# Long convolution by tables: input turned in quarters of its times, half of the forward products replaced by sums, inverses moved by a slot

## The chip, the cores and the metric

One core of a Trainium2 chip runs the program. The metric is the device time of one execution in microseconds (us), the median over several runs. The engines are TensorE (PE; its weight loads are shown apart as PEld), VectorE (DVE), ScalarE (ACT), GpSimd (POOL), and SyncE (SP), which here only issues DMA. Each engine works through its own list of instructions in order and waits on semaphores for the others.

## What is computed

One layer of a model with three parallel groups of heads over 512 latent tokens and 256 context tokens, all in float32. The group that the change touches is a gated long convolution of order two over 512 channels:

```python
def fft_long_conv(z, k_f, bias):
    L = z.shape[1]
    zf = z.astype(jnp.float32)
    y = jnp.fft.irfft(jnp.fft.rfft(zf, n=2 * L, axis=1) * k_f, n=2 * L, axis=1)[:, :L]
    return (y + zf * bias.astype(jnp.float32)).astype(z.dtype)
...
    v, x1, x2 = jnp.split(u, 3, axis=-1)
    z = x1 * fft_long_conv(v, k_f[:, 0], lp["hy_bias"][0])
    return x2 * fft_long_conv(z, k_f[:, 1], lp["hy_bias"][1])
```

The other two groups are attention with compressed keys and a pooling over windows. All three read one projection `h @ w_in` (2048 to 4928 columns) and feed one output projection (2048 by 2048).

## The kernel before

**Precision.** Every large product is done in three passes, with each operand cut into a high part (rounded to the type fp32r by ACT) and a low part (the rest, by a subtraction on DVE): high by high, low by high, high by low. `passes` (L1758 to L1761) issues the three matmuls.

**Slots.** The projection runs as 68 chunks of weights of 128 by 1024. The loop variable `n` of every engine counts these chunks, and this document calls the work written down for one `n` a slot. In a slot ACT makes the high part of chunk n + 1 (`chunk_high`, L630), DVE its low part (`chunk_low`, L1151), and PE multiplies chunk n (`half_chunk`, 24 matmuls of 512 columns at L1730): 12, then the slot's extra work, then 12. PE's chunk n waits for the low part of chunk n; ACT's high part of chunk n + 1 waits until PE has finished chunk n - 1. Everything else is put into slots by hand: each engine has its own list of "if n is this, do that", in the order in which it is done.

**The convolution.** For order o (0, 1) and half of the channels (256 of 512 each), m = 2 o + half. With c = n - TC[o] for the first half and n - TC[o] - 4 for the second (TC = 9, 25), the slots are:

- `transposes` (PE, L1834; c = 0, or -2 for the second half): times come onto the partitions. Even and odd times lie in two banks; a source is read with a step of two floats.
- `turned` (ACT and DVE): high and low part of the transposed input.
- `forward` (PE; c = 1, or 0 for the second half): cosine and sine products (x) of the even and the odd times (pr), for 256 frequencies (two blocks ft) from 256 times (two blocks jt): 16 products of three passes, 48 matmuls of 256 columns.
- `odd_parts` (ACT, L737) copies the odd times' products out of PSUM, `butterflies` (DVE, c = 1, L1246 and L1247) adds and subtracts them, which gives the 256 frequencies and the 256 mirrored ones.
- `filtered` (DVE, c = 2) and `mirrored`, `folded` (DVE, c = 3) multiply by the filter's spectrum and fold; `product_high` (ACT, L752) and `product_low` (DVE, L1287), both c = 4, cut the result in two.
- `inverse` (PE; c = 5 and 6) makes the output of 128 channels each, 24 matmuls of 256 columns, and `outputs` (DVE, same slot, L1297 and L1298) adds and multiplies.

So order 0 has transposes in slots 9 and 11, forward in 10 and 13, inverses in 14, 15, 18, 19; order 1 the same 16 slots later. `neighbour_taps` (DVE, L1176 and L1178) is a short convolution that is put into the slots of `NEIGHBOURS`. `link` lets an engine wait for its own last instruction. SP loads the cosine and sine tables (`fwd_raw`, L377) before the chunks from 3 on; ACT and DVE cut them into parts in slots 3 and 4. In slots 4 to 8 and 20 to 24 the filter's taps and spectrum are made.

Of the kernel before, what the change touches and what calls it, by code (L numbers as in the profile page):

```python
# [61 lines left out]
def backbone(nc, mem, t, out):  # L62
# [6 lines left out]
    with ExitStack() as ctx:  # L69
# [6 lines left out]
        cond, silu_c, spread = alloc("cond", 2 * KT), alloc("silu_c", 2 * KT), alloc("silu_spread", 32 * KT)  # L76
# [18 lines left out]

        shift_x, shift_c = at("shift_x", TMP + 0.5, AW), at("shift_c", TMP + 1.75, 3 * P)
# [6 lines left out]
        inv_hi, inv_raw, inv_lo = at("inv_hi", TAB + 8, 1024, F32R), at("inv_raw", TAB + 10, 1024), at("inv_lo", TAB + 10, 1024, F32R)  # L103
        T = at("temps", TMP, 5 * L)
# [214 lines left out]
        def _(eng):  # L319
# [57 lines left out]
            eng.dma_start(fwd_raw[:], t["tables"][:, 0:2048]).then_inc(tab_in, 16)  # L377
            for n in range(KW, 4 * B_GROUPS):
# [15 lines left out]
                if slot == TC[0] + 9:  # L394
                    eng.wait_ge(mirror_done, 2)
                    load_decay(5)
                    load_decay(6)
# [129 lines left out]
        def _(eng):  # L527
# [204 lines left out]
            def odd_parts(n):  # L732
                for x in range(2):
                    eng.wait_ge(f_mm, 2 * n + x + 1)
                    if n and x == 0:
                        eng.wait_ge(g_lo_done, 4 * n)
                    eng.activation(tmp_of(0) if x else tmp_of(2), ps[2 + 2 * x + 1][:], ACT.Copy).then_inc(f_odd, 1)  # L737
# [8 lines left out]
            def product_high(n):  # L746
                for g in range(4):
                    eng.wait_ge(g_sum, 4 * n + g + 1)
                    if n and g == 0:
                        eng.wait_ge(i_mm, 2 * n)  # L750
                    src = (tmp_of(0), Z[:, 2 * L:3 * L], tmp_of(1), Z[:, 3 * L:4 * L])[g]
                    eng.activation(g_hi[:, g * L:(g + 1) * L], src, ACT.Copy).then_inc(g_hi_done, 1)  # L752
# [134 lines left out]
            for n in range(4 * B_GROUPS):  # L887
# [19 lines left out]
                if n == 12:  # L907
                    eng.wait_ge(tab_in, 32)
                    eng.activation(inv_hi[:], inv_raw[:], ACT.Copy).then_inc(fixed_hi, 1)
                if n == 3:  # L910
                    eng.wait_ge(tab_in, 16)
                    eng.activation(fwd_hi[:], fwd_raw[:], ACT.Copy).then_inc(fixed_hi, 1)
                    sine(1)
# [125 lines left out]
        def _(eng):  # L1039
# [141 lines left out]
            def fixed_low(i):  # L1181

                lo, x, hi = ((w3_lo, w3_raw, w3_hi), (fwd_lo, fwd_raw, fwd_hi), (inv_lo, inv_raw, inv_hi), (w3_lo, w3_raw, w3_hi))[i]
                eng.wait_ge(fixed_hi, i + 1)
                eng.tensor_tensor(lo[:], x[:], hi[:], ALU.subtract).then_inc(fixed_lo, 1)
# [54 lines left out]
            def butterflies(n):  # L1240
                for x in range(2):
                    eng.wait_ge(f_odd, 2 * n + x + 1)
                    if n and x == 0:
                        eng.wait_ge(g_hi_done, 4 * n)
                    odd = tmp_of(0) if x else tmp_of(2)
                    eng.tensor_tensor(Z[:, x * L:(x + 1) * L], ps[2 + 2 * x][:], odd, ALU.add)  # L1246
                    eng.tensor_tensor(Z[:, (2 + x) * L:(3 + x) * L], ps[2 + 2 * x][:], odd, ALU.subtract).then_inc(f_done, 1)  # L1247

            def filtered(n):
                half = n % 2  # L1250
                eng.wait_ge(f_done, 2 * n + 2)
                eng.wait_ge(k_done, 4 * (n // 2) + 4)
                c, s = as2(Z[:, 0:L]), as2(Z[:, L:2 * L])
                kc, ks = halves(K, 0, half), halves(K, 2, half)
                ta, tb = as2(tmp_of(0)), as2(tmp_of(1))
# [4 lines left out]
                eng.tensor_tensor(c, c, tb, ALU.subtract)  # L1260
                link(eng.tensor_tensor(s, s, ta, ALU.add))

            def mirrored(n):
                half = n % 2
                c, s = as2(Z[:, 2 * L:3 * L]), as2(Z[:, 3 * L:4 * L])
                kc, ks = halves(K, 4, half), halves(K, 6, half)
                ta, tb = as2(tmp_of(3)), as2(tmp_of(4))
# [7 lines left out]
            def folded(n):  # L1275
                eng.wait_ge(mirror_done, n + 1)
                for x in range(2):
                    low_, mirror = Z[:, x * L:(x + 1) * L], Z[:, (2 + x) * L:(3 + x) * L]
                    eng.tensor_tensor(tmp_of(x), low_, mirror, ALU.add).then_inc(g_sum, 1)
                    eng.tensor_tensor(mirror, low_, mirror, ALU.subtract).then_inc(g_sum, 1)  # L1280

            def product_low(n):
                for g in range(4):
                    eng.wait_ge(g_sum, 4 * n + g + 1)
                    eng.wait_ge(g_hi_done, 4 * n + g + 1)
                    src = (tmp_of(0), Z[:, 2 * L:3 * L], tmp_of(1), Z[:, 3 * L:4 * L])[g]
                    eng.tensor_tensor(g_lo[:, g * L:(g + 1) * L], src, g_hi[:, g * L:(g + 1) * L], ALU.subtract).then_inc(g_lo_done, 1)  # L1287

            def outputs(o, c):
# [5 lines left out]
                y = ps[6 + c % 2][:].rearrange("p (r t) -> p t r", r=2)  # L1295
                z = u(c).rearrange("p (t r) -> p t r", r=2)
                link(eng.scalar_tensor_tensor(out=z, in0=y, scalar=nrm[:, n:n + 1], in1=z, op0=ALU.mult, op1=ALU.add))  # L1297
# [166 lines left out]
            for n in range(4 * B_GROUPS):  # L1464
# [28 lines left out]
                for o in range(2):  # L1493
# [8 lines left out]
                    for half, c in ((0, n - TC[o]), (1, n - TC[o] - 4)):  # L1502
# [3 lines left out]
                        if c == 1:  # L1506
                            butterflies(m)
                        if c == 2:
                            filtered(m)
                        if c == 3:  # L1510
                            mirrored(m)
                            folded(m)
                        if c == 4:
                            product_low(m)
                        if c in (5, 6):
                            outputs(o, 2 * half + c - 5)
# [130 lines left out]
        def _(eng):  # L1647
# [172 lines left out]
            def transposes(n):  # L1820
# [9 lines left out]
                for b in range(2):  # L1830
                    for jt in range(2):
                        for cc in range(2):
                            src = u(2 * half + cc)[:, b + 256 * jt:256 * (jt + 1):2]
# [3 lines left out]
            def forward(n):  # L1837
# [4 lines left out]
                else:  # L1842
                    eng.wait_ge(k_done, 4 * o + 4)
                for x in range(2):
                    for pr in range(2):
                        for ft in range(2):
                            for jt in range(2):
                                a = (2 * (2 * x + pr) + jt) * 256 + ft * P
                                b = (2 * pr + jt) * 256
                                mm = passes(ps[2 + 2 * x + pr][:, ft * 256:(ft + 1) * 256],  # L1850
                                            (fwd_hi[:, a:a + P], fwd_lo[:, a:a + P]),
                                            (zt_hi[:, b:b + 256], zt_lo[:, b:b + 256]), jt == 0, jt == 1)
                    mm.then_inc(f_mm, 1)
# [23 lines left out]
            for n in range(4 * B_GROUPS):  # L1877
# [3 lines left out]
                for o in range(2):  # L1881
# [7 lines left out]
                    for half, c in ((0, n - TC[o]), (1, n - TC[o] - 4)):  # L1889
# [5 lines left out]
                        if c in (5, 6):  # L1895
                            inverse(o, 2 * half + c - 5)
# [243 lines left out]
def layout(inputs):  # L2140
# [13 lines left out]
    def tile(o):  # L2154
# [12 lines left out]

    w = np.pi * (2 * np.arange(HF) + 1) / (2.0 * L)
    waves = [fn(np.outer(2 * np.arange(HF) + odd, w)) for fn in (np.cos, np.sin) for odd in (0, 1)]
    tables = np.concatenate([m[i * P:(i + 1) * P] for m in waves for i in range(2)]  # L2170
                            + [m.T[i * P:(i + 1) * P] for m in waves[::2] for i in range(2)], axis=1)

    f32 = np.float32
    order = np.concatenate([np.arange(0, L, 2), np.arange(1, L, 2)])
# [69 lines left out]
```

## Time and profile before

| | |
|---|---|
| median of 3 runs | 973.11 us (972.97 to 973.54) |
| the profiled execution | 973.39 us |
| its span | 971.6 us |
| granted clock of PE over the span | 0.997 |
| busy: PE, PEld, DVE, ACT, POOL | 944.4, 780.7, 615.5, 397.7, 97.3 us |

A row of the timeline is: start in us, duration in us, engine, line, operation, output and inputs, shapes, count; in brackets the idle time before it and what ended that. Durations of matmuls overlap their successors, so the distance between starts tells what one costs. DVE's rows overlap a little in the same way. In the waits a row reads: who waits, for what, total us, times, longest. In groups: count, busy us, mean ns of one, idle before.

### The profile page before, as it was taken

Reading aid. Unit: us, or ns where it says so; the run is one execution under the profiler, and the core shown is the slowest. Engines: PE = TensorE matmul, PEld = TensorE weight load, DVE = VectorE, ACT = ScalarE, POOL = GpSimd, SP = SyncE. Lnnn points to the kernel's source line nnn. Section 1 sums busy time; section 2 is a strip of 40 time slices with the busy share of each in tenths; the row PEclk is TensorE's granted clock in tenths of the full one; section 3 lists DMA queues with packets and bytes.
Section 4 is the critical chain, followed back from the end, with each engine's and each line's share of the span. In section 5 each row is a group of like instructions: output and inputs, shape, how many; then the busy total and the mean of one; then the engine's idle time right before and its main releaser. Section 6 shows DMA issues by size and latency. Waiting matters only on the chain.

```text
span 971.6 us, 12485 instructions
## 1 busy us (share of the span) xinstructions
PE 944.4 (97%) x5018; PEld 780.7 (80%) x5018; DVE 615.5 (63%) x805; ACT 397.7 (41%) x625; POOL 97.3 (10%) x78
## 2 busy tenths in 40 slices
PE   5999999999999999999999999999999999999996
PEld 3667777888888889888887788889888888888885
DVE  2766889788756676736785563777777754414254
ACT  3555656354234433323323323645455542212224
POOL 1122200210002200000002360000000000202020
PEclk9999999999999999999999999999999999999998
DMA  9999833222232221258775233101001127222314
GB/s 368 420 422 375 333 128 98 68 84 68 85 96 84 73 78 52 87 167 297 264 283 172 87 129 131 38 18 44 12 1 44 44 88 295 94 87 87 107 67 173
DMA packets 28982, 137.21 MB, mean 141 GB/s; under 512 B 3739, under 2 KB 4059, under 8 KB 21756
## 3 DMA queue, kind: packets, MB, share of 16 engines
q1 hardware_dynamic: 28204, 135.76, 38.9%
q8 instruction: 40, 0.66, 0.3%
q10 hardware_dynamic: 720, 0.65, 0.2%
q14 instruction: 18, 0.15, 0.0%
HBM read 132.20 MB, written 4.19 MB: 140 GB/s over the span
## 4 chain that ended last, share of the span: by engine, by line
PE 81%; DVE 9%; DMA 4%; ACT 4%; issue 2%; POOLq 0%; SPq 0%; ACTq 0%; DVEq 0%
PE pp L1730 32%; PE pp L1760 18%; PE pp L2038 18%; DMA wa_raw<-in_wa_dram 3%; PE pp L1677 3%; PE pp L2001 2%; PE pp L1654 2%; DVE w_lo L1151 1%; PE pp L1681 1%; DMA ada_raw<-in_w_ada_dram 1%; PE pp L1993 1%; PE pp L1992 1%; DVE softmax_stats L1411 1%; DVE pt_lo L1426 1%; ACT U L837 1%
## 5 line engine op out<-in xcount | busy, mean ns | idle before, releaser
L1730 PE MATMUL pp<-h_hi,w_hi 128*128 128x512 f32 x544 | 214.2, 394 | 1.9 <-DVE w_lo L1151 1.2
L1730 PE MATMUL pp<-h_hi,w_lo 128*128 128x512 f32 x544 | 211.9, 390 | 0.0
L1730 PE MATMUL pp<-h_lo,w_hi 128*128 128x512 f32 x544 | 211.9, 389 | 0.0
L1151 DVE TENSOR_TENSOR w_lo<-w_raw,w_hi 128x1024 fp32r<-128x1024 f32 x68 | 87.3, 1284 | 98.4 <-ACT w_hi L630 98.2
L630 ACT ACTIVATE w_hi<-w_raw 128x1024 fp32r<-128x1024 f32 x68 | 71.9, 1058 | 168.2 <-PE pp L1730 120.7
L1730 PEld LDWEIGHTS pp<-h_hi,w_hi 128*128 128x128 f32 x544 | 102.2, 188 | 26.3 <-DVE w_lo L1151 3.6
L1730 PEld LDWEIGHTS pp<-h_hi,w_lo 128*128 128x128 f32 x544 | 102.1, 188 | 21.6
L1730 PEld LDWEIGHTS pp<-h_lo,w_hi 128*128 128x128 f32 x544 | 102.2, 188 | 20.8 <-issue 0.5
L2038 PE MATMUL pp<-wo_hi,m_hi 128*128 128x512 f32 x256 | 100.5, 393 | 0.0
L2038 PE MATMUL pp<-wo_hi,m_lo 128*128 128x512 f32 x256 | 99.6, 389 | 0.0
L2038 PE MATMUL pp<-wo_lo,m_hi 128*128 128x512 f32 x256 | 99.6, 389 | 0.0
L1446 DVE TENSOR_TENSOR wo_lo<-wo_raw,wo_hi 128x2048 fp32r<-128x2048 f32 x16 | 36.7, 2291 | 92.7 <-ACT wo_hi L868 92.7
L868 ACT ACTIVATE wo_hi<-wo_raw 128x2048 fp32r<-128x2048 f32 x16 | 30.6, 1914 | 89.4 <-PE pp L2038 89.4
L2038 PEld LDWEIGHTS pp<-wo_lo,m_hi 128*128 128x128 f32 x256 | 48.1, 188 | 10.4 <-issue 0.5
L2038 PEld LDWEIGHTS pp<-wo_hi,m_hi 128*128 128x128 f32 x256 | 48.1, 188 | 10.3 <-issue 0.5
L2038 PEld LDWEIGHTS pp<-wo_hi,m_lo 128*128 128x128 f32 x256 | 48.0, 188 | 10.1
L519 POOL TENSOR_TENSOR y<-y,gain 128x512 f32<-128x512 f32 x12 | 15.5, 1297 | 339.8 <-ACT out_tmp L875 339.5
L1426 DVE TENSOR_TENSOR pt_lo<-pp,pt_hi 128x768 fp32r<-128x768 f32 x32 | 30.5, 953 | 26.1 <-ACT pt_hi L845 26.0
L845 ACT ACTIVATE pt_hi<-pp 128x768 fp32r<-128x768 f32 x32 | 26.0, 812 | 50.9 <-PE pp L2001 50.9
L1654 PE MATMUL pp<-ada_raw,silu_spread 128*32 128x256 f32 x512 | 34.6, 413 | 7.6 <-DMA ada_raw<-in_w_ada_dram 7.2
L837 ACT ACTIVATE U<-pp,softmax_stats 128x768 f32<-128x768 f32 x32 | 28.9, 903 | 27.8 <-DVE softmax_stats L1413 27.6
L1677 PE MATMUL pp<-a_hi,wa_hi 128*128 128x512 f32 x80 | 35.2, 441 | 2.5 <-DVE a_lo L1055 2.5
(306 smaller groups left out, 1863.2 us busy)
## 6 DMA issues: line engine op xcount, KB each, us to landing
w_raw<-in_wb_dram SPq DMA_DIRECT2D x68, 512.0 KB, 3.6
ada_raw<-in_w_ada_dram SPq DMA_DIRECT2D x15, 2048.0 KB, 13.0
w_gate_raw<-in_w_gate_dram SPq DMA_DIRECT2D x16, 1024.0 KB, 5.0
wo_raw<-in_w_out_dram SPq DMA_DIRECT2D x16, 1024.0 KB, 4.8
wa_raw<-in_wa_dram SPq DMA_DIRECT2D x16, 320.0 KB, 7.7
UG<-in_xT_dram SPq DMA_DIRECT2D x8, 512.0 KB, 8.7
y<-in_x_dram SPq DMA_DIRECT2D x4, 1024.0 KB, 7.8
wh_raw<-in_w_heads_dram SPq DMA_DIRECT2D x4, 768.0 KB, 4.3
```

The lines of the kernel that those rows point to most:

```text
L630: eng.activation(lane(wb_hi, n % 2), lane(wb_raw, n % KW), ACT.Copy).then_inc(wb_hi_done, 1)
L837: eng.activation(prob(n % 3).rearrange("p (a b) -> p a b", a=2), psum[:, 2 * (n % 2):2 * (n % 2) + 2, 0:384], ACT.Exp, bias=st[:, 4 * s + ...
L845: eng.activation(pt_hi[:].rearrange("p (k q) -> p k q", k=6)[:, :, o:o + P], psum[:, 4:6, :].rearrange("p a b -> p (a b)")[:, 0:LK].rearra ...
L868: eng.activation(wo_high_[n % 2][:], wo_raw[n % 3][:], ACT.Copy).then_inc(wo_hi, 1)
L1151: eng.tensor_tensor(lane(wb_lo, n % KW), lane(wb_raw, n % KW), lane(wb_hi, n % 2), ALU.subtract).then_inc(wb_lo_done, 1)
L1426: eng.tensor_tensor(lo, psum[:, 4:6, :].rearrange("p a b -> p (a b)")[:, 0:LK].rearrange("p (k q) -> p k q", k=6), hi, ALU.subtract).then_ ...
L1446: eng.tensor_tensor(wo_low_[n % 3][:], wo_raw[n % 3][:], wo_high_[n % 2][:], ALU.subtract).then_inc(wo_lo, 1)
L1654: mm = eng.matmul(ps[7][32 * strip:32 * strip + 32, 0:256], spread[:, 32 * kk:32 * kk + 32], src[:, kk * 256:(kk + 1) * 256], start=kk < 4 ...
L1677: mm = eng.matmul(ps[i][:], w, x, start=first and n == 0, stop=last and n == 2)
L1730: mm = eng.matmul(ps[i][:], w, x, start=(kk == 0 and m == 0), stop=(kk == KT - 1 and m == 2))
L1760: mm = eng.matmul(dst, w, x, start=first and m == 0, stop=last and m == 2)
L2038: mm = eng.matmul(psum[:, 4 * (b % 2) + tok, :], a, v[:, w:w + L], start=(kk == 0 and m == 0), stop=(kk == 15 and m == 2))
```

## The change

The input is transposed with a step of four floats, so that times 0, 4, 8, ... and 2, 6, 10, ... (and 1, 5, ...; 3, 7, ...) stand in separate blocks. Each block of 128 times is multiplied for 128 frequencies only: 8 products of three passes in place of 16 for each m. New on DVE, `quarter_sums` (c = 1) adds and subtracts these products, and `butterflies` (now c = 2, before `filtered`) makes the 256 frequencies and their mirrored ones. `filtered_sums` (c = 3) holds the last two operations of what was `filtered`, and `folded` moves from c = 3 to c = 4. The tiles T and Z change roles. The inverses and outputs go to slots TC[o] + 6, 7, 9, 10 (before: 5, 6, 9, 10). The inverse writes 256 even times, 128 times 1, 5, 9, ... and 128 times 3, 7, ... in descending order, so `outputs` takes three operations where it took one. A table of 256 columns more is loaded, and cut by ACT and DVE. The short convolutions 6 and 7 go from slot 14 to slot 18. `silu_spread` moves to a place that is free while it is used, which makes room for the new table. The host's tables and the order of the filter's times are laid out to match (not shown); their amount of work is the same.

```diff
 TF, TC = (4, 20), (9, 25)
-NEIGHBOURS = (2, 2, 6, 6, 10, 10, 14, 14, 26, 26, 28, 29)
+NEIGHBOURS = (2, 2, 6, 6, 10, 10, 18, 18, 26, 26, 28, 29)
 GATES = 39
+INVERSE = (6, 7, 9, 10)
...
-        cond, silu_c, spread = alloc("cond", 2 * KT), alloc("silu_c", 2 * KT), alloc("silu_spread", 32 * KT)
+        cond, silu_c = alloc("cond", 2 * KT), alloc("silu_c", 2 * KT)
...
+        spread = at("silu_spread", FREE + 13, 32 * KT)
...
+        last_hi, last_raw, last_lo = at("last_hi", 42.75, 256, F32R), at("last_raw", 43.25, 256), at("last_lo", 43.25, 256, F32R)
...
+        def quarters(x, a, step):
+            y = x[:, a:a + 256]
+            return bass.AP(tensor=y.tensor, offset=y.offset, ap=[list(y.ap[0]), [step, 2], [1, 256]])
+        def descending(x):
+            y = x[:, 0:P]
+            return bass.AP(tensor=y.tensor, offset=y.offset + L - 1, ap=[list(y.ap[0]), [-1, P]])
...
             eng.dma_start(fwd_raw[:], t["tables"][:, 0:2048]).then_inc(tab_in, 16)
+            eng.dma_start(last_raw[:], t["tables"][:, 3072:3328]).then_inc(tab_in, 16)
...
-                    eng.wait_ge(mirror_done, 2)
+                    eng.wait_ge(g_sum, 8)
...
             def odd_parts(n):
                 for x in range(2):
                     eng.wait_ge(f_mm, 2 * n + x + 1)
                     if n and x == 0:
-                        eng.wait_ge(g_lo_done, 4 * n)
-                    eng.activation(tmp_of(0) if x else tmp_of(2), ps[2 + 2 * x + 1][:], ACT.Copy).then_inc(f_odd, 1)
+                        eng.wait_ge(g_sum, 4 * n)
+                    eng.activation(as2(tmp_of(x)), psum[:, 2 + 2 * x:4 + 2 * x, 256:512], ACT.Copy).then_inc(f_odd, 1)
...
-                    eng.wait_ge(tab_in, 32)
+                    eng.wait_ge(tab_in, 48)
                     eng.activation(inv_hi[:], inv_raw[:], ACT.Copy).then_inc(fixed_hi, 1)
                 if n == 3:
-                    eng.wait_ge(tab_in, 16)
+                    eng.wait_ge(tab_in, 32)
+                    eng.activation(last_hi[:], last_raw[:], ACT.Copy)
...
+                if i == 1:
+                    eng.tensor_tensor(last_lo[:], last_raw[:], last_hi[:], ALU.subtract)
...
-            def butterflies(n):
+            def quarter_sums(n):
                 for x in range(2):
                     eng.wait_ge(f_odd, 2 * n + x + 1)
                     if n and x == 0:
-                        eng.wait_ge(g_hi_done, 4 * n)
-                    odd = tmp_of(0) if x else tmp_of(2)
-                    eng.tensor_tensor(Z[:, x * L:(x + 1) * L], ps[2 + 2 * x][:], odd, ALU.add)
-                    eng.tensor_tensor(Z[:, (2 + x) * L:(3 + x) * L], ps[2 + 2 * x][:], odd, ALU.subtract).then_inc(f_done, 1)
+                        eng.wait_ge(g_lo_done, 4 * n)
+                    first, second = psum[:, 2 + 2 * x:4 + 2 * x, 0:256], as2(tmp_of(x))
+                    eng.tensor_tensor(quarters(Z, x * 256, L), first, second, ALU.add)
+                    if x == 0:
+                        eng.tensor_tensor(quarters(Z, 2 * L, 768), first, second, ALU.subtract).then_inc(f_done, 1)
+                    else:
+                        eng.tensor_tensor(Z[:, 2 * L + 256:3 * L], tmp_of(1)[:, 0:256], ps[4][:, 0:256], ALU.subtract)
+                        eng.tensor_tensor(Z[:, 3 * L:3 * L + 256], ps[5][:, 0:256], tmp_of(1)[:, 256:512], ALU.subtract).then_inc(f_done, 1)
+            def butterflies(n):
+                eng.wait_ge(f_done, 2 * n + 2)
+                for ft in range(2):
+                    even, odd = as2(Z[:, 2 * ft * L:(2 * ft + 1) * L]), as2(Z[:, (2 * ft + 1) * L:(2 * ft + 2) * L])
+                    eng.tensor_tensor(quarters(T, ft * 256, L), even, odd, ALU.add)
+                    ins = eng.tensor_tensor(quarters(T, 2 * L + ft * 256, L), even, odd, ALU.subtract)
+                link(ins)
...
             def filtered(n):
                 half = n % 2
-                eng.wait_ge(f_done, 2 * n + 2)
                 eng.wait_ge(k_done, 4 * (n // 2) + 4)
-                c, s = as2(Z[:, 0:L]), as2(Z[:, L:2 * L])
+                c, s = as2(tmp_of(0)), as2(tmp_of(1))
                 kc, ks = halves(K, 0, half), halves(K, 2, half)
-                ta, tb = as2(tmp_of(0)), as2(tmp_of(1))
+                ta, tb = as2(Z[:, 0:L]), as2(Z[:, L:2 * L])
                 eng.tensor_tensor(ta, c, ks, ALU.mult)
                 link(eng.tensor_tensor(tb, s, ks, ALU.mult))
                 eng.tensor_tensor(c, c, kc, ALU.mult)
                 link(eng.tensor_tensor(s, s, kc, ALU.mult))
-                eng.tensor_tensor(c, c, tb, ALU.subtract)
-                link(eng.tensor_tensor(s, s, ta, ALU.add))
+            def filtered_sums(n):
+                eng.tensor_tensor(tmp_of(0), tmp_of(0), Z[:, L:2 * L], ALU.subtract)
+                link(eng.tensor_tensor(tmp_of(1), tmp_of(1), Z[:, 0:L], ALU.add))
...
-                c, s = as2(Z[:, 2 * L:3 * L]), as2(Z[:, 3 * L:4 * L])
+                c, s = as2(tmp_of(2)), as2(tmp_of(3))
                 kc, ks = halves(K, 4, half), halves(K, 6, half)
-                ta, tb = as2(tmp_of(3)), as2(tmp_of(4))
+                ta, tb = as2(Z[:, 2 * L:3 * L]), as2(Z[:, 3 * L:4 * L])
...
-                    low_, mirror = Z[:, x * L:(x + 1) * L], Z[:, (2 + x) * L:(3 + x) * L]
-                    eng.tensor_tensor(tmp_of(x), low_, mirror, ALU.add).then_inc(g_sum, 1)
-                    eng.tensor_tensor(mirror, low_, mirror, ALU.subtract).then_inc(g_sum, 1)
+                    low_, mirror = tmp_of(x), tmp_of(2 + x)
+                    eng.tensor_tensor(Z[:, x * L:(x + 1) * L], low_, mirror, ALU.add).then_inc(g_sum, 1)
+                    eng.tensor_tensor(Z[:, (2 + x) * L:(3 + x) * L], low_, mirror, ALU.subtract).then_inc(g_sum, 1)
...
-                y = ps[6 + c % 2][:].rearrange("p (r t) -> p t r", r=2)
-                z = u(c).rearrange("p (t r) -> p t r", r=2)
-                link(eng.scalar_tensor_tensor(out=z, in0=y, scalar=nrm[:, n:n + 1], in1=z, op0=ALU.mult, op1=ALU.add))
+                y, z = ps[6 + c % 2], u(c)
+                for a, x in ((z[:, 0::2], y[:, 0:256]), (z[:, 1::4], y[:, 256:384]), (z[:, 3::4], descending(y))):
+                    ins = eng.scalar_tensor_tensor(out=a, in0=x, scalar=nrm[:, n:n + 1], in1=a, op0=ALU.mult, op1=ALU.add)
+                link(ins)
                 eng.tensor_tensor(u(c), u(c), u(4 + c), ALU.mult).then_inc(y_done, 1)
...
                         if c == 1:
+                            quarter_sums(m)
+                        if c == 2:
                             butterflies(m)
-                        if c == 2:
                             filtered(m)
                         if c == 3:
+                            filtered_sums(m)
                             mirrored(m)
+                        if c == 4:
                             folded(m)
-                        if c == 4:
                             product_low(m)
-                        if c in (5, 6):
-                            outputs(o, 2 * half + c - 5)
+                    if n - TC[o] in INVERSE:
+                        outputs(o, INVERSE.index(n - TC[o]))
...
-                            src = u(2 * half + cc)[:, b + 256 * jt:256 * (jt + 1):2]
+                            src = u(2 * half + cc)[:, b + 2 * jt::4]
...
-                        for ft in range(2):
-                            for jt in range(2):
-                                a = (2 * (2 * x + pr) + jt) * 256 + ft * P
-                                b = (2 * pr + jt) * 256
-                                mm = passes(ps[2 + 2 * x + pr][:, ft * 256:(ft + 1) * 256],
-                                            (fwd_hi[:, a:a + P], fwd_lo[:, a:a + P]),
-                                            (zt_hi[:, b:b + 256], zt_lo[:, b:b + 256]), jt == 0, jt == 1)
+                        for jt in range(2):
+                            a, b = (2 * (2 * x + pr) + jt) * 256, (2 * pr + jt) * 256
+                            hi, lo = fwd_hi[:, a:a + P], fwd_lo[:, a:a + P]
+                            if pr and jt:
+                                hi, lo = last_hi[:, x * P:(x + 1) * P], last_lo[:, x * P:(x + 1) * P]
+                            mm = passes(ps[2 + 2 * x + pr][:, jt * 256:(jt + 1) * 256], (hi, lo),
+                                        (zt_hi[:, b:b + 256], zt_lo[:, b:b + 256]), True, True)
...
-                            inverse(o, 2 * half + c - 5)
+                    if n - TC[o] in INVERSE:
+                        inverse(o, INVERSE.index(n - TC[o]))
...
```

## Rows read from the trace of the kernel before

**Rows 1.** Windows over both convolutions, columns: us, busy of PE, PEld, DVE, ACT, POOL
```profile
205.00:289.30 84.30, 83.63 (x465) 72.61 (x464) 62.04 (x88) 33.44 (x48) 0.00 (x0) 1.00 0.28 86
...
334.20:418.20 84.00, 83.34 (x463) 72.42 (x462) 58.84 (x85) 28.25 (x40) 0.00 (x0) 1.00 0.22 67
```
**Rows 2.** Waits of PE over the whole span: us, times, longest
```profile
PE pp L1730 <- DVE w_lo L1151: 1.2, 2, 0.6
```
**Rows 3.** Groups by form: the forward products' first pass, and the loads for transposes
```profile
L1760 PE MATMUL pp<-zt_hi,fwd_hi 128*128 128x256 f32 x64 | 18.1, 283 | 0.0
...
L2001 PEld LDWEIGHTS pp<-ident,U 128*128 128x128 f32 x192 | 22.8, 140 | 4.4 <-DVE U L1420 2.5
...
L1834 PEld LDWEIGHTS pp<-ident,U 128*128 128x128 f32 x32 | 4.3, 207 | 1.1 <-ACT hy_small L946 1.0
```
**Rows 4.** Timeline of PE, slots 10 to 18 of the first convolution: start, duration
```profile
212.50 0.28 PE L1760 MATMUL pp<-zt_hi,fwd_hi 128*128 128x256 f32 x1
...
218.25 0.40 PE L1730 MATMUL pp<-h_hi,w_hi 128*128 128x512 f32 x1
...
223.73 1.11 PE L1834 MATMUL pp<-ident,U 128*128 128x128 f32 x8
...
224.60 0.48 PE L1730 MATMUL pp<-h_hi,w_hi 128*128 128x512 f32 x1
...
258.06 0.40 PE L1730 MATMUL pp<-h_hi,w_hi 128*128 128x512 f32 x1
...
272.44 0.50 PE L1730 MATMUL pp<-h_hi,w_hi 128*128 128x512 f32 x1 [0.60 <-DVE w_lo L1151]
...
275.34 0.28 PE L1760 MATMUL pp<-inv_hi,g_hi 128*128 128x256 f32 x1
```
**Rows 5.** Timeline of DVE in slots 8 to 17
```profile
202.94 0.41 DVE L1123 TENSOR_TENSOR U<-U 128x256 f32<-128x256 f32 x1
203.27 0.68 DVE L1122 TENSOR_TENSOR U<-U,rstd 128x512 f32<-128x512 f32 x1
...
213.06 1.23 DVE L1151 TENSOR_TENSOR w_lo<-w_raw,w_hi 128x1024 fp32r<-128x1024 f32 x1 [2.83 <-ACT w_hi L630]
214.20 0.75 DVE L1176 SCALAR_TENSOR_TENSOR U<-UG,par,U 128x511 f32<-128x511 f32 x1
...
217.10 0.68 DVE L1246 TENSOR_TENSOR z_spec<-pp,temps 128x512 f32<-128x512 f32 x1
...
224.09 0.69 DVE L1257 TENSOR_TENSOR temps<-z_spec,spectrum 128x512 f32<-128x512 f32 x1
224.81 0.69 DVE L1258 TENSOR_TENSOR z_spec<-z_spec,spectrum 128x512 f32<-128x512 f32 x1
225.42 0.68 DVE L1259 TENSOR_TENSOR z_spec<-z_spec,spectrum 128x512 f32<-128x512 f32 x1
...
249.92 0.75 DVE L1297 SCALAR_TENSOR_TENSOR U<-pp,nrm,U 128x512 f32<-128x512 f32 x1 [0.32 <-PE pp L1760]
250.70 0.69 DVE L1298 TENSOR_TENSOR U<-U 128x512 f32<-128x512 f32 x1
...
271.17 1.22 DVE L1151 TENSOR_TENSOR w_lo<-w_raw,w_hi 128x1024 fp32r<-128x1024 f32 x1
```
**Rows 6.** Timeline of ACT, slots 11 and 13
```profile
221.26 1.06 ACT L630 ACTIVATE w_hi<-w_raw 128x1024 fp32r<-128x1024 f32 x1 [2.21 <-PE pp L1730]
...
236.20 0.63 ACT L752 ACTIVATE g_hi<-temps 128x512 fp32r<-128x512 f32 x1 [1.98 <-DVE temps L1279]
```
**Rows 7.** Timeline of SP, ACT, DVE and PE where the tables are loaded and rounded
```profile
127.00 0.33 SPq L377 DMA_DIRECT2D fwd_raw<-in_tables_dram  x1
...
153.48 1.92 ACT L912 ACTIVATE fwd_hi<-fwd_raw 128x2048 fp32r<-128x2048 f32 x1
...
157.18 0.63 ACT L695 ACTIVATE z_spec<-z_spec 64x512 f32<-64x512 f32 x1 [1.78 <-DVE z_spec L1197]
...
167.31 1.22 DVE L1219 TENSOR_TENSOR tap_lo<-z_spec,tap_hi 128x1024 fp32r<-128x1024 f32 x1 [1.20 <-ACT tap_hi L712]
...
169.16 0.39 PE L1760 MATMUL pp<-tap_hi,fwd_hi 128*128 128x512 f32 x1
```

More of the change, by code:

```diff
@@ L750, in product_high @@
                         eng.wait_ge(i_mm, 2 * n)
-                    src = (tmp_of(0), Z[:, 2 * L:3 * L], tmp_of(1), Z[:, 3 * L:4 * L])[g]
+                    src = Z[:, (0, 2, 1, 3)[g] * L:((0, 2, 1, 3)[g] + 1) * L]
                     eng.activation(g_hi[:, g * L:(g + 1) * L], src, ACT.Copy).then_inc(g_hi_done, 1)
@@ L1285, in product_low @@
                     eng.wait_ge(g_hi_done, 4 * n + g + 1)
-                    src = (tmp_of(0), Z[:, 2 * L:3 * L], tmp_of(1), Z[:, 3 * L:4 * L])[g]
+                    src = Z[:, (0, 2, 1, 3)[g] * L:((0, 2, 1, 3)[g] + 1) * L]
                     eng.tensor_tensor(g_lo[:, g * L:(g + 1) * L], src, g_hi[:, g * L:(g + 1) * L], ALU.subtract).then_inc(g_lo_done, 1)
@@ L1894, in _ @@
                             forward(m)
-                        if c in (5, 6):
-                            inverse(o, 2 * half + c - 5)
+                    if n - TC[o] in INVERSE:
+                        inverse(o, INVERSE.index(n - TC[o]))
                 if n == GATES + KT + 1:
@@ L2168, in layout @@
     w = np.pi * (2 * np.arange(HF) + 1) / (2.0 * L)
-    waves = [fn(np.outer(2 * np.arange(HF) + odd, w)) for fn in (np.cos, np.sin) for odd in (0, 1)]
-    tables = np.concatenate([m[i * P:(i + 1) * P] for m in waves for i in range(2)]
-                            + [m.T[i * P:(i + 1) * P] for m in waves[::2] for i in range(2)], axis=1)
+    mirror = np.concatenate([np.arange(0, HF, 2), np.arange(HF - 1, 0, -2)])
+    fours = np.concatenate([np.arange(0, HF, 2), np.arange(1, HF, 2)])
+    waves = [fn(np.outer(2 * np.arange(HF) + odd, w))[:, mirror] for fn in (np.cos, np.sin) for odd in (0, 1)]
+    rows = [m[mirror if i % 2 else fours] for i, m in enumerate(waves)]
+    tables = np.concatenate([m[i * P:(i + 1) * P] for m in rows for i in range(2)]
+                            + [m.T[i * P:(i + 1) * P] for m in waves[::2] for i in range(2)]
+                            + [m[1::2, 0:P] for m in waves[1::2]], axis=1)
     f32 = np.float32
-    order = np.concatenate([np.arange(0, L, 2), np.arange(1, L, 2)])
+    order = np.concatenate([2 * fours, 2 * mirror + 1])
     tt = np.linspace(0.0, 1.0, L, dtype=f32)[:, None]
```

## The prediction

> **What bounds the kernel now.** I read the windows first. Over each of the two convolutions PE is busy for all but 0.66 us (84.30 less 83.63, 84.00 less 83.34), and its clock stands at 1.00, the 2.4 GHz level; DVE has 22.3 and 25.2 us without work, ACT over 50 [rows 1]. So in these stretches the time is what PE has to issue, plus the few places where it waits. The waits say where these are: PE waited twice, 0.6 us each, for a chunk's low part from DVE [rows 2]. The timeline puts the first at 272.44, chunk 18 [rows 4], whose low part DVE made from 271.17 [rows 5], with slot 16's multiplications and `folded` queued ahead of it; the other is in the same place of the second convolution. Hence two readings are needed: what a removed matmul is worth, and whether DVE, which gets more work, stays ahead of PE in each slot.
>
> What a matmul is worth is the distance of starts, not its duration (283 ns, [rows 3]), since they overlap. The 48 of one `forward` go from 212.50 to 218.25: 5.75 us, 0.120 each. A slot's 24 large ones go from 218.25 to 223.73: 5.48 us. The 8 transposes go from 223.73 to 224.60: 0.87 us [rows 4].
>
> **Removed from PE.** Each `forward` has 24 matmuls in place of 48: 24 x 0.120 = 2.88 us, four times: 11.5 us. All 192 of the three passes (64 a pass, [rows 3]) stand in stretches in which PE has no gap, so this lies wholly on the path. The inverses keep their 24 matmuls (2.9 us) and only move.
>
> **The old waits.** From 258.06 to 275.34 stand 72 large matmuls, 16.44 us at the rate above; they took 17.28 [rows 4]. So the wait of 0.60 with its slow restart costs 0.84 us, twice. The change takes `folded` (4 operations) out of that slot, so the cause goes, if DVE isn't later for another reason.
>
> **DVE, slot by slot.** An unlinked operation of 512 columns costs 0.61 us, one of 256 0.33, a `link` 0.11 more, a chunk's low part 1.14, a scaled sum of 512 columns with its link 0.78, four short-convolution operations 2.90 [rows 5]. Between the 256 and 512 columns a column costs 1.1 ns, so a scaled sum takes about 0.40 for 256 and 0.27 for 128, and with its link `outputs` costs 1.05 in place of 0.78 for the sum; with the product (0.6) 1.65. `quarter_sums` is 3 x 0.61 + 2 x 0.33 = 2.5, as long as the old butterflies (4 x 0.61 = 2.4). The new `butterflies` adds 2.4 and a link. For each convolution DVE gets 2 x 2.6 + 4 x 0.27 = 6.3 us more, and PE's stretch gets about 6.4 us shorter: DVE would be busy about 68 us of 78. It has room on average; the places count. ACT starts a chunk's high part 0.29 us after PE's slot begins (220.97, which is 218.25 and half of 5.48; 221.26 in [rows 6]), and DVE follows 1.1 later.
>
> From 212.50, first convolution: slot 11 begins at 218.1, 12 at 224.5, 13 at 229.9, 14 at 238.3, 15 at 243.7, 16 at 252.1, 17 at 260.4, 18 at 265.9 (a slot is 5.44 to 5.48, plus 2.9 with a forward or inverse, 0.9 with transposes). DVE: the quarter sums of slot 10 end at 217.10 + 2.5 = 219.6. Slot 11 has the low part (to 220.7), `butterflies` and `filtered` (8 operations, 3 links: 5.2) and `turned` (1.2): 227.1. Slot 12 waits for ACT until 227.5, low part 13 is there at 228.6 for 229.9; eight operations more: 233.8. Slot 13: low part 14 at 235.0, the inverse table's 1.14, `folded` 2.4, `product_low` 2.4: 240.9. Low part 15 is there at 242.1 for 243.7. Slot 15 ends at 253.0, slot 16 at 261.9, low part 18 is there at 263.1 for 265.9, and the products' low parts at 267.9, where the third inverse wants them at 268.6. So no wait, with 1.3, 1.6 and 0.7 us to spare. `product_high` on ACT now comes after `folded` in the same slot: ACT sits behind DVE (as at 236.20, [rows 6]) and chunk 15's high part starts about 1 us late, at 239.3; this stands in the walk, since DVE is busy until 240.9 anyway.
>
> In the second convolution the same walk, 129.0 later, has two short-convolution operations (1.45) more in slots 28 and 29 and no inverse table: low part 31 is there at 372.4 for 372.6. That is the tightest place: 0.2 us. I take no wait there, and keep 0 to 1 us.
>
> **Moved.** Inverses 0 and 1 go from slots 14, 15 to 15, 16, the others stay. The outputs wait only for them; 1 and 0 are needed by transposes nine slots later. Short convolutions 6 and 7 add 2.9 us in slot 18; there DVE would wait from 269.0 (low part 19) to 271.5 (the third inverse's end) anyway, which takes 2.5 of it; `outputs` 2 and 3 need them right behind, in slots 18 and 19. The decays' loads on SP wait for `folded` (slot 17) in place of `mirrored`, behind chunk 20's load, which itself waits for chunk 17: nothing later is held up.
>
> **Tables.** The further table is issued on SP right behind the one at 127.00; ACT rounds that at 153.48, so the new 128 KB has over 20 us. ACT's further copy (about 0.35) falls ahead of `sine`, where ACT waited 1.78 us for DVE. DVE's further 0.33 makes the first tap's low part end at 168.9 in place of 168.5, and PE wants it at 169.16 [rows 7]. Nothing, with 0.3 to spare. `silu_spread` only changes its address.
>
> **Transposes.** They now read every fourth float. The trace has no such load: those with a step of one take 140 ns, with a step of two 207 [rows 3], and the starts are 0.109 apart [rows 4]. Bounds: nothing, or a load of twice 207 ns of whose longer half only 0.1 us is hidden, so 0.1 more for each transpose: 0.8 per group of 8, 3.2 in all. I take 0.4 us in all, since the step from one to two, half again as long a load, has left the distance near 0.11.
>
> The Trainium skill ("SBUF — State Buffer", section "Door 1: The DMA port swizzle") speaks against this edit: it says that SBUF has lines of 16 bytes and that each access that goes to a new line pays. Four floats are a line, so every read of the new transposes would pay, where every second one did; by it the sum would take the upper bound. That 207 stands against 140 already agrees in kind; no row shows the size.
>
> **Sum.** 11.5 + 1.7 - 0.4 = 12.8 us. The profiled execution took 973.39 (span 971.6 and 1.8 around it), so 960.6; against the median of 973.11: 960.3. Behind slot 35 all work is tied to slots, so it moves up as a whole.
>
> **Rivals.** (a) DVE's new forms (two pieces of 256, a step of 2 or 4 floats, a falling step) are a quarter slower. They make up 13.6 us per convolution (2 x 4.9 and 4 x 0.94), so 3.4 more, about 1.9 of it ahead of low part 31 (0.2 spare) or 15 (1.6 spare) and 1.1 ahead of the third inverse: about 3 us of waits in all, 963.3. For: the spare time is thin. Against: `filtered` already reads pieces of 256 at 0.61, and `outputs` reads PSUM with a step of 256 at the price of a plain scaled sum (0.75 against 0.75, [rows 5]). (b) The transposes cost the upper bound: 963.1. (c) PE's freed time comes back in part as waits in several slots, since ACT and DVE wait for each other more than in my walk: 964 to 971. Against: DVE has 10 us free in each stretch. (d) Slower: the new forms take twice as long. Then 13.6 us per convolution come on top, 7.4 of them in slots 10 to 14 with at most 1.6 spare, and some 4.3 in 15 to 17, of which about 2 go into DVE's waits for ACT: 8 to 9 us of waits per convolution, 17 in all, 977. It turns the sign from about 75% longer operations. The same rows as for (a) speak against it. (e) Nothing is gained, because the matmuls weren't what PE's time went into: 973. [Rows 4] exclude it nearly: no gap in 48 matmuls.
>
> **Chances.** The forecast 0.72 (its own range 959.3 to 961.5: waits of 0 to 1, transposes of 0 to 0.8), (a) 0.11, (b) 0.07, (c) 0.05, (d) 0.03, (e) 0.02. Up to 963.4 the range takes in (a) and (b); below, 959.0 holds a sum without costs, and 0.8 for what I haven't seen. A measurement tells 0.2% (1.9 us) from no change; that gives faster 0.95, same 0.02, slower 0.03.
>
> **What would show it.** Right: 96 matmuls in place of 192 with fwd_hi as weights and zt inputs, 2.9 us for 24; the waits for low parts of chunks 18 and 34 gone; the start of the taps' first product in slot 20 some 6.2 us earlier relative to slot 10, and again in the second convolution; DVE busy near 68 us of 78. The forecast is wrong if PE waits for low part 31, for `product_low` ahead of an inverse, or if a group of 8 transposes takes over 1.1 us; if `butterflies` shows steps of over 0.65 us, it is (a) or (d).

## The result

The changed kernel takes 960.30 us (median of 4 runs, 959.71 to 960.68) against 973.28 us before: ratio 0.9857, 95% interval 0.9841 to 0.9874. That is 13.0 us less, faster, and the forecast (960.3).

The first part of the profile page after the change:

```profile
span 957.9 us, 12330 instructions
PE 932.2 (97%) x4922; PEld 770.0 (80%) x4922; DVE 627.8 (66%) x842; ACT 397.7 (42%) x626; POOL 97.5 (10%) x78
```

PE has 96 matmuls fewer (4922 against 5018). The windows over the two convolutions, 77.6 us long now (columns as in [rows 1]):

```profile
205.00:282.60 77.60, 77.53 (x417) 66.98 (x416) 68.02 (x105) 33.02 (x49) 0.00 (x0) 1.00 0.26 91
327.40:405.00 77.60, 77.53 (x417) 66.98 (x416) 64.77 (x103) 28.06 (x41) 0.00 (x0) 1.00 0.21 70
```

DVE is busy 68.0 and 64.8 us of them, 6 us more than in [rows 1]. PE is without work for 0.07 us where it was 0.66. In the waits of PE over the whole span the row of [rows 2] has gone; what is left near the convolutions is

```profile
PE pp L1803 <- DVE tap_lo L1241: 0.9, 1, 0.9
...
PE pp L1773 <- ACT UG L652: 0.6, 1, 0.6
```

which stand in slots 8 and 4 and were there before.

**Where the time went.** Two distances in PE's timeline hold it all. The first runs from the first forward matmul to the first matmul of the taps in slot 20, the second from the third forward to the last matmul of the last inverse. Before (the start of the first one is in [rows 4]):

```profile
292.02 0.39 PE L1785 MATMUL pp<-w_hi,filter_hidden 128*128 128x512 f32 x1
...
341.46 0.28 PE L1760 MATMUL pp<-zt_hi,fwd_hi 128*128 128x256 f32 x1
...
415.34 0.28 PE L1760 MATMUL pp<-fwd_hi,g_lo 128*128 128x256 f32 x1
```

After:

```profile
212.25 0.28 PE L1803 MATMUL pp<-zt_hi,fwd_hi 128*128 128x256 f32 x1
...
215.13 0.40 PE L1773 MATMUL pp<-h_hi,w_hi 128*128 128x512 f32 x1
...
220.60 1.12 PE L1877 MATMUL pp<-ident,U 128*128 128x128 f32 x8
...
221.48 0.47 PE L1773 MATMUL pp<-h_hi,w_hi 128*128 128x512 f32 x1
...
257.48 0.40 PE L1773 MATMUL pp<-h_hi,w_hi 128*128 128x512 f32 x1
...
268.39 0.28 PE L1803 MATMUL pp<-inv_hi,g_hi 128*128 128x256 f32 x1
...
285.07 0.39 PE L1828 MATMUL pp<-w_hi,filter_hidden 128*128 128x512 f32 x1
...
334.52 0.28 PE L1803 MATMUL pp<-zt_hi,fwd_hi 128*128 128x256 f32 x1
...
401.77 0.28 PE L1803 MATMUL pp<-fwd_hi,g_lo 128*128 128x256 f32 x1
```

The first distance went from 79.52 to 72.82 us, the second from 73.88 to 67.25: 6.70 + 6.63 = 13.3 us. A forward takes 2.88 us (212.25 to 215.13) where it took 5.75; the 48 matmuls from 257.48 to 268.39 take 0.227 each without a wait, where the 72 of [rows 4] took 0.240. The rest of the span, and the 49.4 us between the two distances, stayed. The profiled executions differ by 13.7 us in their spans (971.6 and 957.9); the 0.4 us beyond the distances lie ahead of the first forward and behind the last inverse. In what follows these distances are used beside the medians, since they repeat within 0.02 us from one execution of the changed kernel to the next (72.84 and 67.25 in another), while the total varies by some 2 us, of which the last section tells what the traces show.

DVE's queue at the tight places, after the change:

```profile
240.65 1.21 DVE L1171 TENSOR_TENSOR w_lo<-w_raw,w_hi 128x1024 fp32r<-128x1024 f32 x1
...
244.90 1.23 DVE L1171 TENSOR_TENSOR w_lo<-w_raw,w_hi 128x1024 fp32r<-128x1024 f32 x1 [0.58 <-ACT w_hi L648]
246.04 0.68 DVE L1283 TENSOR_TENSOR temps<-z_spec 128x512 f32<-128x512 f32 x1
246.65 0.69 DVE L1284 TENSOR_TENSOR temps<-z_spec 128x512 f32<-128x512 f32 x1
...
261.84 1.22 DVE L1171 TENSOR_TENSOR w_lo<-w_raw,w_hi 128x1024 fp32r<-128x1024 f32 x1
...
265.39 2.49 DVE L1326 TENSOR_TENSOR g_lo<-z_spec,g_hi 128x512 fp32r<-128x512 f32 x4
...
364.19 1.22 DVE L1171 TENSOR_TENSOR w_lo<-w_raw,w_hi 128x1024 fp32r<-128x1024 f32 x1
```

Low part 15 (240.65), 18 (261.84) and 31 (364.19) are ready at 241.9, 263.1 and 365.4, and the second `product_low` at 267.9. PE wants them at 243.5, 265.7, 365.8 and 268.4 (half a slot ahead of the inverse at 268.39 is 265.67). The new `butterflies` step by 0.61 us like any other operation.

### The profile page after: what moved, and what is told of

It is laid out like the page before. It is cut to its first block, busy times and chain, and to the rows that moved or that the text cites. A ratio compares the mean times of both kernels' runs of the same rounds, so it can differ in the third digit from the quotient of the medians.

```text
span 957.9 us, 12330 instructions
## 1 busy us (share of the span) xinstructions
PE 932.2 (97%) x4922; PEld 770.0 (80%) x4922; DVE 627.8 (66%) x842; ACT 397.7 (42%) x626; POOL 97.5 (10%) x78
## 4 chain that ended last, share of the span: by engine, by line
PE 86%; DVE 6%; DMA 3%; ACT 3%; issue 1%; SPq 0%; POOLq 0%; ACTq 0%; DVEq 0%
PE pp L1773 35%; PE pp L2082 18%; PE pp L1803 17%; PE pp L1720 4%; PE pp L1697 2%; PE pp L2045 2%; DMA wa_raw<-in_wa_dram 2%; DMA ada_raw<-in_w_ada_dram 1%; PE pp L1724 1%; PE pp L2037 1%; PE pp L2036 1%; DVE softmax_stats L1452 1%; DVE pt_lo L1467 1%; ACT U L856 1%; PE pp L1877 0%
```

## The experiments

"First" and "second" below are the two distances; those of the changed kernel are 72.82 and 67.25.

**1. `folded` moved alone**, in the kernel before:

```diff
                         if c == 3:
                             mirrored(m)
-                            folded(m)
                         if c == 4:
+                            folded(m)
                             product_low(m)
```

> The kernel before, with nothing changed but `folded` moved from c = 3 to c = 4, ahead of `product_low`. Theory (PE is the bound, and waits only where DVE's queue makes a low part late): the two waits for the low parts of chunks 18 and 34 go (0.92 us each, 1.8 in all). But DVE's queue then ends `product_low` at the same moment as before, 274.8, and the third inverse, now wanted at 274.4, waits for it 0.4 us, in each convolution. So 973.3 - 1.8 + 0.9 = 972.4. Rival 1: the waits go and nothing else is late: 971.5. Rival 2: the waits have another cause than `folded`: 973.3, with the wait at the start of chunk 18 as before.

Measured: 972.50 us, ratio 0.9988 (0.9979 to 0.9997); first 79.02, second 73.43, so 0.50 and 0.45 us less than before. The waits of PE, slots 6 to 39, and the place in its timeline:

```profile
PE pp L1760 <- DVE g_lo L1287: 0.3, 2, 0.2
```
```profile
274.36 0.39 PE L1730 MATMUL pp<-h_hi,w_lo 128*128 128x512 f32 x1
274.91 0.39 PE L1760 MATMUL pp<-inv_hi,g_hi 128*128 128x256 f32 x1 [0.16 <-DVE g_lo L1287]
275.13 0.28 PE L1760 MATMUL pp<-inv_lo,g_hi 128*128 128x256 f32 x1
```

The waits for the low parts are gone, and a wait for `product_low` stands in their place: of 1.8 us only half is gained. The number in brackets understates what a wait costs. The starts lie 0.55 us apart where 0.23 is usual, and the next ones 0.22 where 0.12 is usual (the slow restart): 0.42 us are lost for 0.16 in brackets. The theory holds to 0.1 us, both rivals fall.

**2. Every forward product twice**, in the changed kernel:

```diff
-                            mm = passes(ps[2 + 2 * x + pr][:, jt * 256:(jt + 1) * 256], (hi, lo),
+                            for _ in range(2):
+                                mm = passes(ps[2 + 2 * x + pr][:, jt * 256:(jt + 1) * 256], (hi, lo),
...
```

> The changed kernel, with every forward product issued twice into the same place, so that PE has again 48 matmuls in a forward (same result). Everything else as changed. Theory: the matmuls' time lies wholly on the path: 960.3 + 4 x 24 x 0.120 = 971.8. Rival: part of the gain comes from elsewhere and DVE's longer queue eats into it, so that PE's spare time hides part of the second issue: below 970.

Measured: 971.57 us (0.9976, 0.9967 to 0.9985); first 78.60, second 73.00: 5.78 and 5.75 us more. So 11.5 us are the matmuls, wholly on the path. What is left to the kernel before (79.52 less 78.60, 73.88 less 73.00) is 0.92 and 0.88, which I put down to the old waits. The rows agree: the 72 matmuls that took 17.28 us in [rows 4] would take 16.37 at the 0.227 of the changed kernel, 0.91 less. With this the 13.3 us are accounted for.

**3. `folded` back at c = 3**, in the changed kernel (the edit of 1 turned round):

> The changed kernel with `folded` back at c = 3, behind `mirrored`. Theory (walk along DVE's queue): low part 18 is there at about 265.4 for 265.7, low part 30 at 360.4 for 360.4, low part 34 at 387.7 for 388.0, so nothing or up to 0.3 us is lost: 960.3 to 960.6. Rival: `folded` in that slot is the cause of the old waits whatever else stands there: 1.8 us come back, 962.1, with waits for the low parts of chunks 18 and 34.

Measured: 961.00 us (0.9868, 0.9855 to 0.9881); first 72.94, second 67.70: 0.12 and 0.45 us more. The matmuls show no wait, the weight loads ahead of them do (waits of PEld, slots 10 to 38, then its timeline at chunks 18, 30 and 34):

```profile
PEld pp L1773 <- DVE w_lo L1171: 0.9, 3, 0.5
```
```profile
266.32 0.19 PEld L1773 LDWEIGHTS pp<-h_hi,w_hi 128*128 128x128 f32 x1 [0.24 <-DVE w_lo L1171]
...
361.38 0.19 PEld L1773 LDWEIGHTS pp<-h_hi,w_hi 128*128 128x128 f32 x1 [0.47 <-DVE w_lo L1171]
...
389.04 0.19 PEld L1773 LDWEIGHTS pp<-h_hi,w_hi 128*128 128x128 f32 x1 [0.23 <-DVE w_lo L1171]
```

They are the three places that the walk named, chunk 30 the longest, and the loss is a third of the rival's 1.8 us (0.6 where up to 0.3 was expected). So `folded` alone wasn't the cause of the old wait: what counts is the sum of what stands ahead of a low part, and in the changed kernel the four operations nearly fit.

Part of that sum was no work at all. In the kernel before, the `outputs` of slot 15 stood ahead of `filtered`, and DVE stood still until the inverse was done:

```profile
258.26 0.75 DVE L1297 SCALAR_TENSOR_TENSOR U<-pp,nrm,U 128x512 f32<-128x512 f32 x1 [3.22 <-PE pp L1760]
```

From there to low part 18 (271.17, [rows 5]) its queue has no gap. The change puts `outputs` behind the rest of a slot, and between 236 and 275 us DVE of the changed kernel stands still for 1.1 us in all. These 3.2 us are more than the 0.9 by which low part 18 came late, so this order is a second candidate for what removed the old wait. No run changed it alone, and its share isn't shown.

**4. Three operations more on DVE**, ahead of low parts 15 and 31:

```diff
+                if n in (14, 30):
+                    for _ in range(3):
+                        link(eng.tensor_tensor(tmp_of(4), K[:, 0:L], K[:, L:2 * L], ALU.add))
                 if n + 1 < 4 * B_GROUPS:
                     chunk_low(n + 1)
```

> The changed kernel with three linked operations of 512 columns (0.72 us each, 2.2 in all, into a free tile) put on DVE ahead of the low parts of chunks 15 and 31. Theory: these are the places with the least to spare (1.6 us for chunk 15, 0.4 for chunk 31 by the changed kernel's timeline), so PE waits about 0.6 and 1.8 us there and restarts slowly: 960.3 + 2.6 = 962.9. Rival: DVE has 10 us without work in each convolution and takes 2.2 more without a loss: 960.3.

Measured: 963.45 us (0.9896, 0.9882 to 0.9910); first 73.54 (0.72 more), second 69.21 (1.96 more). The waits stand at the two chunks:

```profile
244.48 0.50 PE L1776 MATMUL pp<-h_hi,w_hi 128*128 128x512 f32 x1 [0.37 <-DVE w_lo L1171]
...
368.74 0.50 PE L1776 MATMUL pp<-h_hi,w_hi 128*128 128x512 f32 x1 [1.65 <-DVE w_lo L1171]
```

2.7 us lost for 4.3 us of work on an engine with 10 us free in each stretch: what counts is what is spare ahead of the next low part.

**5. Inverses early**, `INVERSE = (5, 6, 9, 10)` in the changed kernel:

> The changed kernel with the inverses 0 and 1 and their outputs back in slots TC + 5 and TC + 6. Theory: in the first convolution `product_low` ends at 240.7, just when the inverse of slot 14 would begin (240.8): no wait. In the second it ends at 364.3 and the inverse of slot 30 would begin at 363.1, because two short convolutions stand ahead of it on DVE: PE waits 1.2 us: 961.6. Rival 1: the later slot wasn't needed: 960.3. Rival 2: both convolutions wait, and chunk 31's low part as well: 963 or more.

Measured: 963.28 us (0.9886, 0.9872 to 0.9901); first 73.58 (0.76 more), second 69.24 (1.99 more). Three waits where one was expected (waits of PE, then its timeline):

```profile
PE pp L1803 <- DVE g_lo L1326: 1.9, 3, 1.0
```
```profile
269.53 0.39 PE L1803 MATMUL pp<-inv_hi,g_hi 128*128 128x256 f32 x1 [0.43 <-DVE g_lo L1326]
...
365.55 0.39 PE L1803 MATMUL pp<-inv_hi,g_hi 128*128 128x256 f32 x1 [1.04 <-DVE g_lo L1326]
```

The 1.04 is the one foretold. The other two, 0.43 each, stand at the third inverse of both convolutions. With the early inverse PE's slot 14 is 2.9 us longer, so ACT's high part of chunk 16 comes that much later. DVE has only the first `outputs` (1.8 us), now in slot 14, to put in between, and then stands still for ACT:

```profile
245.92 0.69 DVE L1339 TENSOR_TENSOR U<-U 128x512 f32<-128x512 f32 x1
248.35 1.23 DVE L1171 TENSOR_TENSOR w_lo<-w_raw,w_hi 128x1024 fp32r<-128x1024 f32 x1 [1.73 <-ACT w_hi L648]
```

In the changed kernel that wait is 0.58 (244.90 above). The 1.1 us that DVE loses here it lacks for the second `product_low`, which had 0.5 to spare. So moving the inverses by a slot is worth 2.7 us, about twice the 1.3 that I gave it before the run, and 1.5 of it (0.76 in each convolution) lies at the third inverses, which weren't moved.

**6. Short convolutions 6 and 7 back in slot 14** (`NEIGHBOURS`, 18 to 14):

> The changed kernel with the short convolutions 6 and 7 back in slot 14. Theory: DVE's 2.9 us more push its queue until 0.9 us of waits for ACT are used up; low parts 16, 17 and 18 are still in time (264.5 for 265.7), but `product_low` ends at 269.4 where the third inverse wants it at 268.4: about 1.0 us and a slow restart, 961.5. Rival: DVE catches up and nothing is lost: 960.3.

Measured: 961.32 us (0.9866, 0.9851 to 0.9880); first 74.03 (1.21 more), second 67.24 (unchanged), with the wait at the third inverse as foretold:

```profile
269.67 0.39 PE L1803 MATMUL pp<-inv_hi,g_hi 128*128 128x256 f32 x1 [0.93 <-DVE g_lo L1326]
```

**7. Transposes reading neighbouring floats:**

```diff
-                            src = u(2 * half + cc)[:, b + 2 * jt::4]
+                            src = u(2 * half + cc)[:, (b + 2 * jt) * P:(b + 2 * jt + 1) * P]
```

> The changed kernel with the transposes reading 128 neighbouring floats in place of every fourth (so the convolution gets other times in its blocks; same count and size of everything). Theory: a read with a step costs PE almost nothing, the 8 transposes take 0.78 us in place of 0.88: 959.9. Rival (each read that goes to a new line of 16 bytes pays, on the path): the groups of 8 become much shorter than 0.88 and the time falls to 958 or below.

Measured: 960.22 us (0.9860, 0.9843 to 0.9876). The loads for the transposes, groups of PEld, in the changed kernel:

```profile
L1877 PEld LDWEIGHTS pp<-ident,U 128*128 128x128 f32 x32 | 4.4, 210 | 1.1 <-ACT hy_small L966 1.0
```

and in this one:

```profile
L1877 PEld LDWEIGHTS pp<-ident,U 128*128 128x128 f32 x32 | 3.6, 141 | 1.2 <-ACT hy_small L966 1.0
```

The four groups of 8 transposes take 0.99, 0.88, 0.99, 0.88 us with a step of four, 0.98, 0.87, 0.98, 0.87 with a step of two (the kernel before), and 0.85, 0.79, 0.84, 0.79 with a step of one: any step costs 0.5 us in all, the step of four 0.04 more than that of two. So the theory holds and the rival falls; a median can't show a gain of 0.5 us (last section).

**8. `outputs` on neighbouring floats** (the three pieces written to 0:256, 256:384, 384:512 of the tile; the falling read stays):

> The changed kernel with the three operations of `outputs` working on neighbouring floats of the output tile (the results go to other times; the falling read of PSUM stays). In the changed kernel the pieces of 128 take 431 to 446 ns and the one of 256 (step of two) 482, while by the rows of before (0.75 for 512, 1.07 ns per column) they should take 0.35 and 0.48. Theory: the step of four floats costs DVE about 0.09 us for 128 elements: the 128 ones fall to 0.35, those of 256 stay. Rival 1: it is a floor for such short operations: they stay at 0.44. Rival 2: the falling read costs it: only one of the two falls. The time stays at 960.3 by all of them, since DVE has 0.3 us to spare behind each.

Measured: 959.97 us (0.9869, 0.9844 to 0.9893), first 72.83, second 67.25. The groups of `outputs` on DVE in the changed kernel:

```profile
L1337 DVE SCALAR_TENSOR_TENSOR U<-pp,nrm,U 128x128 f32<-128x128 f32 x16 | 6.3, 442 | 0.0
...
L1337 DVE SCALAR_TENSOR_TENSOR U<-pp,nrm,U 128x256 f32<-128x256 f32 x8 | 3.9, 482 | 7.8 <-PE pp L1803 7.8
```

and here:

```profile
L1337 DVE SCALAR_TENSOR_TENSOR U<-pp,nrm,U 128x128 f32<-128x128 f32 x16 | 4.8, 342 | 0.0
L1337 DVE SCALAR_TENSOR_TENSOR U<-pp,nrm,U 128x256 f32<-128x256 f32 x8 | 3.9, 482 | 8.0 <-PE pp L1803 7.9
```

Only the pieces with a step of four fall, by 100 ns for 128 elements; a step of two and a falling read cost nothing. The theory holds, both rivals fall, and the time stays as expected.

**9. A better version.** Short convolutions 2 and 3 go from slot 6 to the end of slot 9 on DVE (`if n == 9`, `NEIGHBOURS` 6 to 9). It was run twice, the second time beside the changed kernel:

> The changed kernel with the short convolutions 2 and 3 moved from slot 6 to the end of slot 9 on DVE. Theory: the one wait left in slots 5 to 36, 0.86 us for the taps' low part in slot 8 (about 1.0 with the restart), comes from these 2.9 us ahead of the taps in DVE's queue, while DVE waits 2.8 us for ACT behind slot 9: 960.3 - 1.0 = 959.3. Rival 1: the taps are late for ACT's sake: 960.3 with the wait unchanged. Rival 2: low part 11 becomes late: above 960.3.

> The changed kernel itself, to have it beside the other two on the same chip: 960.3 (959.7 to 960.7 in its first runs).

> The short convolutions 2 and 3 in slot 9 once more, beside the changed kernel. Theory: 1.0 us under the changed kernel. The profiled execution of the first run took 961.9 with three waits for chunks' low parts (2.2 us) that the timed ones can't have had, if they come from chance (a late load of weights): then the median is 959.3 again. Rival: the waits belong to the kernel: 960.3 to 961.9.

Measured: 959.41 us (0.9851, 0.9834 to 0.9867), then 959.16 (0.9845, 0.9823 to 0.9868) beside 960.94 for the changed kernel (0.9853, 0.9830 to 0.9876). No wait is left between slots 6 and 36, and the first forward begins at 211.06 and 211.13 where the changed kernel has 212.25 and 212.55. The profiled executions of both had three waits for low parts in slots 46 to 55 (2.2 and 2.6 us); the changed kernel has such waits in one of its two traces too (last section). The gain of a microsecond is plain in the timeline; the medians agree with it, though their intervals overlap.

**10. The other wait.** On top of 9, ACT copies out the first tile ahead of the sine, in slot 3:

```diff
+                    evacuate(0)
                     sine(1)
```

> As e10, and ACT copies out the first projected tile (evacuate(0), slot 3) ahead of the sine that waits for DVE, in place of behind it. Theory: PE's wait of 0.63 us at the start of chunk 4 (for that copy), 0.9 with the restart, goes, since ACT stood idle 1.78 us ahead of the sine: 959.3 - 0.9 = 958.4. Rival: the sine comes later and with it the first taps, and PE waits there instead: 959.3 or more.

Measured: 959.44 us (0.9841, 0.9824 to 0.9858). The 0.63 at chunk 4 is gone, and PE waits at the first taps instead:

```profile
168.70 0.50 PE L1804 MATMUL pp<-tap_hi,fwd_hi 128*128 128x512 f32 x1 [0.33 <-DVE tap_lo L1242]
```

PE reached these taps 0.8 us earlier and gave back nearly all: the rival holds. DVE's work for the first taps, not ACT's copy, sets the time of slots 3 to 5.

## Why the prediction was right

**Removed from PE:** 2.88 us a forward, 11.5 in all: 2.88 and 2.87 in the timeline, 11.53 put back in experiment 2. The distance of starts was the right price; the durations (283 ns each) would have given 27 us.

**The old waits:** put at 0.84 each, they were 0.92 and 0.88, and are gone. The prediction took 0.228 us for an undisturbed large matmul, and it is 0.227. That they had a cause in DVE's queue is shown by experiment 1, and that moving `folded` alone brings only half by the wait that followed it. The prediction named `folded` as the cause; experiment 3 shows that in the changed kernel it would have brought back 0.6 of 1.8 us, so something else in the change helps too. The moved `outputs` are the candidate, and that part is open.

**DVE, slot by slot:** the walk stands against the trace, its times turned to the changed kernel's clock (0.25 us earlier in the first convolution, 6.94 in the second). Low part 15: 241.8 walked, 241.9 found. Low part 18: 262.8, 263.1. `product_low`: 267.6, 267.9. Low part 31: 365.5, 365.4, with 0.4 to spare where I had 0.2. The error of 0.3 comes from `outputs`, twice: its sum takes 1.22 with its link, not 1.05, because the two pieces with a step of four take 0.1 us more each than with a step of one (experiment 8). It didn't reach the path. Experiments 4 and 6 put load where the walk says that little is spare, and PE waited there, by 0.1 to 0.25 us less than walked (0.37 and 1.65 for 0.6 and 1.8, 0.93 for 1.0).

**Moved:** here the prediction was thin. It said that the outputs only wait for the inverses, and gave the step no price. Experiment 5 shows 2.7 us that would have been lost without it, 1.04 of waiting in slot 30 and 0.43 at each third inverse, besides slow restarts. **Tables** cost nothing, as said: slots 2 to 8 keep their times.

**Transposes:** this term was mis-sized. It stood at 0.4 us, with 3.2 as the upper bound; it is 0.04. The old read with a step of two had already paid. Without it the sum would have been 13.2 (13.3 in the timeline, 13.0 between the medians). So it is luck that 960.3 was met to the tenth: two terms were 0.5 us too pessimistic together, and another series of the same kernel had its median at 960.94. The sentence of the Trainium skill on 16-byte lines ("SBUF — State Buffer", "Door 1: The DMA port swizzle") fits DVE: a step of two floats is free there and a step of four is not (0.342 us for 128 elements with a step of one, 0.442 with four). The same section gives 4 fp32 as how far one can stride for free; the measurement decides against that for a step of four. For PE's weight loads it doesn't hold in this form: a step of two takes them from 140 to 207 ns already, and a step of four adds only 3.

Of the rivals, (a) and (d) fall by the 0.61 us steps of the new forms of 512 columns. Only the pieces of `outputs` with a step of four are longer, 442 ns where 342 is the price of a step of one, and there are too few of them to cost PE anything. The others fall, (b) by 0.88 us for 8 transposes, (c) by 0.07 us of idle PE, (e) by experiment 2.

## What to carry to other kernels

On a queue that is full, price a matmul by the distance of starts and take the other engines slot by slot against the moment at which each of their results is wanted: an engine with 10 us free in 78 had 0.4 us to spare at one place, and 2.2 us of work put there cost 2.0. When work is moved to an earlier slot, look at where its engine next stands still for someone else; time that it doesn't use before that standstill is lost, and the bill comes several slots later. When a wait goes, compute which result is late next before counting the whole wait as a gain (0.95 of 1.8 us here).

## What the runs showed of the hardware

Where the loads of the gate's weights run beside those of the projection (issued in slots 37 to 53), one execution of the same kernel has waits of PE and another has none. In one execution of the changed kernel ACT waited 29.9 us in all for `w_raw` between 440 and 520 us, and PE never; in another ACT waited longer and PE twice:

```profile
ACT w_hi L648 <- DMA w_raw<-in_wb_dram: 50.5, 12, 6.2
```
```profile
472.17 0.50 PE L1773 MATMUL pp<-h_hi,w_hi 128*128 128x512 f32 x1 [0.44 <-DVE w_lo L1171]
...
485.52 0.50 PE L1773 MATMUL pp<-h_hi,w_hi 128*128 128x512 f32 x1 [1.13 <-DVE w_lo L1171]
```

The first of these executions took 959.71 us, the second 962.46. The same kernel took 959.9 to 962.5 us in the second one's series, so a single total can't tell differences of 1 us; the distances in the timeline can. What makes the loads late wasn't tried.

A step of four floats in the output and one input of a scaled sum on DVE costs 0.1 us for 128 elements, a falling read from PSUM nothing (experiment 8). A weight load of 128 by 128 floats takes 141, 207 and 210 ns with steps of one, two and four (experiment 7).
